# A one-core transformer kernel: each weight split placed by hand in the attention stages, values weighed in two banks in cross, the bias masked a stage earlier

## The chip, the cores and the metric

One NeuronCore of a Trainium2 chip runs the whole program in one launch. The metric is the device time of that launch in microseconds (us). Besides TensorE (PE), VectorE (DVE), ScalarE (ACT) and GpSimd (POOL), the sync engine (SP) issues the loads of the weights.

## The reference

Inputs and outputs are float32: x has 256 rows of 1024. Three transformer layers follow each other. Cut to what matters:

```python
x = x + rms_norm(concat(spatial_gating(za), moba_attention(q, k, v), conformer_conv(zc)) @ w_out, g)   # stage moba
x = x + rms_norm(memory_cross_attention(rms_norm(x, g), rms_norm(mem, g), w_xq, w_xkv, w_xo), g)       # cross: 4 heads of 256
x = x + rms_norm(square(relu(rms_norm(x, g) @ w_ff1)) @ w_ff2, g)                                      # relu
for i in range(2):
    x = x + 0.5 * rms_norm(swiglu(rms_norm(x, g), ...), g)                                             # glu0, glu2
    x = x + rms_norm(differential attention of 8 heads (i = 0) or neighbourhood attention of 16 (i = 1), g)  # diff, near
    x = x + 0.5 * rms_norm(swiglu(...), g)                                                             # glu1, glu3
```

Differential attention takes for each head two softmaxes, p0 - lambda * p1, weighs v with it and normalises the result. Neighbourhood attention adds a bias from a table (`na_rpb`) to the scores, and leaves out all keys outside a window.

## The kernel before

The nine stages (moba, cross, relu, glu0, diff, glu1, glu2, near, glu3) run one after the other. All weights come in 226 "chunks" of 128 x 2048 numbers (1 MB). SP loads chunk c into `raw`, one of 7 places, once chunk c - 7 has been used. Each chunk is then split so that products keep float32's accuracy: ACT copies it to `w_hi` (L612, one of 4 places, so it waits until chunk c - 4 has been used), and DVE writes `w_lo` = `raw` - `w_hi` in place over `raw` (L841). PE multiplies three times, hi by hi, lo by hi, hi by lo (L1169 to L1171). A chunk of the attention stages is used in two halves of 12 matmuls, for rows 0 to 127 and for rows 128 to 255 of x; `qc0.0` in the plan is the first half of a chunk of q's weights, `o1.1` the second half of the out product's chunk 1.

The order of everything is written out by hand in `PLAN`, one string of words for each stage. Every engine walks the same string and does what a word asks of it, waiting on semaphores for the others. Besides the chunks, these words matter here:

- `s`: both engines split the next chunk (ACT hi, DVE lo); `h`: only ACT's half; `l`: only DVE's half. Both count chunks by themselves.
- For an attention unit u (a head): `S` scores (PE), `M` their maximum (DVE, L1031), `E` exp (ACT, L671), `N` probabilities (DVE, L1053), `P` their transposes (PE, L1235), `Q` copy to `probT` (ACT, L679), `W` values weighed (PE, L1250 or L1258 or L1271), `O` the result split to `yT_hi` (ACT) and `yT_lo` (DVE, L1080). In diff also `A` squares (ACT), `B` norm (POOL, then DVE), `Z` transposes of the result (PE).
- `rq`, `rk`, `rv`: rows of q, k or v leave PSUM on ACT; in diff DVE then turns q and k by the rotary angles (L1095 to L1101, "rope"); `tq`, `tk`: their transposes (PE, L1401) and ACT's copy of these.
- `post`, `gain`, `sq`, `turn`: the norms between two stages. `conv_out`: the convolution's Silu (ACT, L716), its hi part (ACT, L719) and lo part (DVE) into the tiles of yT which only the out product's chunk 3 reads.

`attention()` and `attention_pairs()` write the words of the units: step s of diff holds O of unit s - 5, then S of s, W of s - 3, P of s - 2, M, A, Q, E, N, B, the chunks given for that step in `fill`, and Z of s - 4. `used_up` counts the chunks that a step ends, and the next step gets as many splits, all at one place: in diff and cross `s` between B (or N) and the chunks. cross gives all values to one PSUM bank, `OUT_BANK`, so W of unit u waits for `O` of unit u - 1. The bias of near is loaded by POOL in 128 small DMAs during relu, glu0, glu1 and glu2, and masked by POOL in near's head (16 instructions, L592).

Of the kernel before, what the change touches and what calls it, by code (L numbers as in the profile page):

```python
# [40 lines left out]


def attention(kind, units, fill, carry=0):

    words = []
    last = 5 if kind == "diff" else 3
    for s in range(units + last):
        def unit(names, lag):  # L50
            words.extend(f"{name}{s - lag}" for name in names if 0 <= s - lag < units)
        early, _, late = fill.get(s, "").rpartition("|")
        if kind == "diff":
            unit("O", 5)
            if s == units + last - 1:
                break
        unit("S", 0)
        unit("W", 3)
        words += early.split()
        unit("P", 2)  # L60
        unit("M", 0)
        unit("A" if kind == "diff" else "O", 3)
        unit("Q", 2)
        unit("E", 0)
        unit("N", 1)
        if kind == "diff":
            unit("B", 3)
        words += ["s"] * carry
        chunks = late.split()
        words += chunks  # L70
        carry = used_up(early.split() + chunks)
        if kind == "diff":
# [4 lines left out]
def attention_pairs(pairs, fill, carry=0):

    words = []
    for s in range(pairs + 2):
        early, _, late = fill.get(s, "").rpartition("|")
        if s >= 2:
            words += [f"W{s - 2}"]
        if 0 <= s - 1 < pairs:
            words += [f"P{2 * s - 2}"]
        if s < pairs:
            words += [f"S{s}"]
        words += early.split()  # L90
        if 0 <= s - 1 < pairs:
            words += [f"P{2 * s - 1}"]
        if s >= 2:
            words += [f"O{s - 2}"]
        if 0 <= s - 1 < pairs:
            words += [f"Q{2 * s - 2}", f"Q{2 * s - 1}"]
        words += ["h"] * carry
        if s < pairs:
            words += [f"{name}{2 * s + j}" for name in "MEN" for j in range(2)]
        words += ["l"] * carry + late.split()  # L100
        carry = used_up(early.split() + late.split())
    return " ".join(words + ["s"] * carry) + " "

# [11 lines left out]
HEAD_QK = ("qa0.0 post1 s qb0.0 gain1 s sq1 rq0.0 ka0.0 turn1 kb0.0 tq0.0 rk0.0 qa0.1 s qb0.1 tk0.0 rq0.1 s ka0.1 "  # L115
           "tq0.1 s kb0.1 rk0.1 s va0.0 tk0.1 va0.1 s ")
PLAN = {
    "moba": ("g0 s a0 s mem s glu consts u0 s lambda taps0 w0 s gate_norm taps1 K0 s taps2 K1 s gate_scale taps3 K2 s "
             "taps4 K3 s mix taps5 V0 s mix_raw taps6 V1 s taps7 V2 s V3 s conv_mean mix_out conv_sq q0 s conv_var "
             "k0 s conv_root v0 " +  # L120
             attention_pairs(4, {0: "q1", 1: "conv_out k1", 2: "v1", 3: "o0", 4: "o3.0|o3.1", 5: "o1.0"}, 1) +
             "o2.0 post0 gain0 o1.1 turn0 sq0 o2.1"),
    "cross": ("qa0.0 post1 s qb0.0 gain1 s sq1 rq0.0 qc0.0 turn1 qd0.0 tq0.0 rq1.0 qa0.1 s qb0.1 tq1.0 rq0.1 s qc0.1 "
              "tq0.1 s qd0.1 rq1.1 s " +
              attention("cross", 4, {0: "tq1.1|", 4: "o0.0", 5: "o0.1", 6: "o1.0"}) +
              "o2.0 o3.0 post0 gain0 o1.1 s o2.1 turn0 sq0 o3.1"),
    "relu": RELU + "post0 gain0 da6.1 s db6.1 turn0 sq0 s da7.1 db7.1",
    "glu0": GLU + "post0 gain0 da4.1 s db4.1 turn0 sq0 d5.1",
    "diff": (HEAD_QK +
             attention("diff", 8, {0: "vb0 rv0", 1: "qc0 qd0.0", 2: "qd0.1 rq1 kc0.0 tq1 kc0.1",  # L130
# [5 lines left out]
    "near": (HEAD_QK +
             attention_pairs(8, {0: "vb0 rv0", 1: "qc0 qd0.0", 2: "qd0.1 rq1 kc0.0 tq1 kc0.1",
                                 3: "kd0.0 rk1.0 kd0.1 tk1.0 rk1.1 vc0.0 tk1.1", 4: "vc0.1 vd0.0", 5: "vd0.1 rv1 o0.0",
                                 6: "o0.1", 7: "o1.0", 8: "o1.1|o2.0a", 9: "o2.0b"}) +
             "o3.0 post0 gain0 o2.1 turn0 sq0 o3.1"),  # L140
# [1393 lines left out]
```

## Time and profile before

| | |
|---|---|
| median of 3 runs | 1458.69 us (1457.83 to 1461.46) |
| the profiled execution | 1458.49 us, span 1456.7 us |
| PE busy, share of the span | 1394.8 us, 96% |
| DVE, ACT, POOL busy | 839.3, 703.8, 145.9 us |
| mean granted clock of TensorE | 0.991 |

How to read it: a matmul's busy time overlaps the next one's, and its end is modelled, so a busy share of 96% does not say that 4% is all that PE loses. Idle time of PE before an instruction, with the engine that released it, is in the view of the waits; the granted clock is 1 at 2.4 GHz and 0.5 at 1.2 GHz.

### The profile page before, as it was taken

Reading aid. Unit: us, or ns where it says so; the run is one execution under the profiler, and the core shown is the slowest. Engines: PE = TensorE matmul, PEld = TensorE weight load, DVE = VectorE, ACT = ScalarE, POOL = GpSimd, SP = SyncE. Lnnn points to the kernel's source line nnn. Section 1 sums busy time; section 2 is a strip of 40 time slices with the busy share of each in tenths; the row PEclk is TensorE's granted clock in tenths of the full one; section 3 lists DMA queues with packets and bytes.
Section 4 is the critical chain, followed back from the end, with each engine's and each line's share of the span. In section 5 each row is a group of like instructions: output and inputs, shape, how many; then the busy total and the mean of one; then the engine's idle time right before and its main releaser. Section 6 shows DMA issues by size and latency. Waiting matters only on the chain.

```text
span 1456.7 us, 17560 instructions
## 1 busy us (share of the span) xinstructions
PE 1394.8 (96%) x7129; PEld 1166.2 (80%) x7129; DVE 839.3 (58%) x904; ACT 703.8 (48%) x908; POOL 145.9 (10%) x248
## 2 busy tenths in 40 slices
PE   6999989999999999997799999999999999999996
PEld 6998778788888888876678888888888866788885
DVE  4978646645565444654665545655455768655452
ACT  5647454544445434564545343553434566543441
POOL 1000101100001110100111010010100700000000
PEclk9999999999999999999999999999999999999998
DMA  9843334765548556552347656576565534365540
GB/s 314 269 161 136 131 130 143 239 200 187 182 156 252 193 193 195 171 173 88 101 130 225 205 181 206 164 220 205 183 204 168 194 116 131 105 233 197 180 138 30
DMA packets 123421, 255.86 MB, mean 176 GB/s; under 512 B 6280, under 2 KB 36812, under 8 KB 123340
## 3 DMA queue, kind: packets, MB, share of 16 engines
q1 hardware_dynamic: 119244, 251.58, 53.3%
q0 software_dynamic: 4096, 3.15, 0.8%
q8 instruction: 57, 0.93, 0.3%
q14 instruction: 24, 0.20, 0.1%
HBM read 253.66 MB, written 1.05 MB: 175 GB/s over the span
## 4 chain that ended last, share of the span: by engine, by line
PE 88%; DVE 4%; ACT 4%; issue 2%; DMA 1%; POOL 0%; SPq 0%; DVEq 0%; POOLq 0%; ACTq 0%
PE ps L1169 26%; PE ps L1171 26%; PE ps L1170 26%; PE ps L1432 2%; ACT w_hi L612 2%; DVE w_lo L841 1%; ACT t L671 1%; PE ps L1157 1%; PE ps L1159 1%; PE ps L1158 1%; PE ps L1235 1%; PE ps L1198 1%; PE ps L1188 1%; DVE top L1031 1%; DMA raw<-w_in 1%
## 5 line engine op out<-in xcount | busy, mean ns | idle before, releaser
L841 DVE TENSOR_TENSOR w_lo<-raw,w_hi 128x2048 fp32r<-128x2048 f32 x226 | 521.0, 2309 | 435.6 <-ACT w_hi L612 435.1
L612 ACT CAST w_hi<-raw 128x2048 fp32r<-128x2048 f32 x226 | 430.2, 1908 | 393.0 <-PE ps L1171 383.1
L1169 PE MATMUL ps<-w_hi,hT_hi 128*128 128x512 f32 (+1 forms) x1168 | 444.2, 380 | 0.3
L1171 PE MATMUL ps<-w_hi,hT_lo 128*128 128x512 f32 (+1 forms) x1168 | 438.2, 375 | 0.0
L1170 PE MATMUL ps<-w_lo,hT_hi 128*128 128x512 f32 (+1 forms) x1168 | 437.7, 375 | 0.0
L1169 PE MATMUL ps<-w_hi,yT_hi 128*128 128x512 f32 (+1 forms) x672 | 258.8, 385 | 3.5 <-DVE yT_lo L1080 2.0
L1171 PE MATMUL ps<-w_hi,yT_lo 128*128 128x512 f32 (+1 forms) x672 | 255.6, 380 | 0.0
L1170 PE MATMUL ps<-w_lo,yT_hi 128*128 128x512 f32 (+1 forms) x672 | 255.3, 380 | 0.0
L1169 PEld LDWEIGHTS ps<-w_hi,hT_hi 128*128 128x128 f32 x1168 | 220.9, 189 | 41.7 <-DVE w_lo L841 3.7
L1171 PEld LDWEIGHTS ps<-w_hi,hT_lo 128*128 128x128 f32 x1168 | 220.9, 189 | 39.9
L1170 PEld LDWEIGHTS ps<-w_lo,hT_hi 128*128 128x128 f32 x1168 | 221.1, 189 | 37.1
L1169 PEld LDWEIGHTS ps<-w_hi,yT_hi 128*128 128x128 f32 x672 | 126.9, 189 | 27.8 <-DVE w_lo L841 4.3
L1171 PEld LDWEIGHTS ps<-w_hi,yT_lo 128*128 128x128 f32 x672 | 126.7, 189 | 24.4
L1170 PEld LDWEIGHTS ps<-w_lo,yT_hi 128*128 128x128 f32 x672 | 126.9, 189 | 22.8
L534 POOL DMA_DIRECT2D big<-na_rpb x128 | 66.1, 518 | 498.4 <-PE ps L1171 498.4
L546 POOL TENSOR_SCALAR rstd<-ssq 128x1 f32<-128x1 f32 x38 | 17.3, 455 | 659.5 <-ACT probT L618 641.7
L793 ACT ACTIVATE att_bias<-ps,rstd 128x512 f32<-128x512 f32 (+1 forms) x64 | 42.5, 664 | 70.7 <-PE ps L1171 70.6
L1114 DVE SCALAR_TENSOR_TENSOR prob<-ps,rstd,att_bias 128x512 f32<-128x512 f32 (+1 forms) x64 | 45.6, 714 | 26.4 <-PE ps L1171 17.1
L879 DVE SCALAR_TENSOR_TENSOR t<-ps,gain 128x512 f32<-128x512 f32 x36 | 24.7, 690 | 42.5 <-ACT probT L618 42.5
L618 ACT ACTIVATE probT<-ps 128x512 f32<-128x512 f32 x36 | 21.5, 597 | 48.8 <-PE ps L1171 48.8
L636 ACT CAST hT_hi<-ps 128x512 fp32r<-128x512 f32 x36 | 19.8, 589 | 46.6 <-PE ps L1188 46.0
L1122 DVE TENSOR_TENSOR yT_lo<-ps,yT_hi 128x512 fp32r<-128x512 f32 (+1 forms) x64 | 38.9, 648 | 2.9 <-ACT yT_hi L799 2.9
(154 smaller groups left out, 1063.9 us busy)
## 6 DMA issues: line engine op xcount, KB each, us to landing
raw<-ffn_wg SPq DMA_DIRECT2D x44, 1024.0 KB, 5.5
raw<-ffn_wu SPq DMA_DIRECT2D x44, 1024.0 KB, 5.5
raw<-ffn_wd SPq DMA_DIRECT2D x44, 1024.0 KB, 5.3
raw<-w_ff SPq DMA_DIRECT2D x32, 1024.0 KB, 5.9
raw<-diff_w_in SPq DMA_DIRECT2D x12, 1024.0 KB, 5.1
raw<-na_w_in SPq DMA_DIRECT2D x12, 1024.0 KB, 5.2
raw<-w_in SPq DMA_DIRECT2D x10, 1024.0 KB, 5.8
raw<-w_xkv SPq DMA_DIRECT2D x8, 1024.0 KB, 10.9
```

The source lines that it names most:

```text
L534: pool.dma_start(bias[p:p + 1], bass.AP(rpb.tensor, (5 - r) * 31 + 15 - c, [[465, 16], [31, 6], [1, 64]])).then_inc(bias_in, 16)
L612: act.copy(hi_part(c), raw[:, c % NRAW, :]).then_inc(hi_done, 1)
L618: act.activation(dump[:, b, :], src, ACT.Square, scale=1.0 / 32, accum_out=acc).then_inc(done, 1)
L793: act.activation(gate[:, t, 0:width], src[:, 0:width], ACT.Relu if kind == "relu" else ACT.Silu, scale=rstd[:, k:k + 1]).then_inc(gate_don ...
L841: dve.tensor_tensor(lo_part(c), raw[:, c % NRAW, :], hi_part(c), ALU.subtract).then_inc(lo_done, 1)
L879: dve.scalar_tensor_tensor(t1[:, t, half_row], ps[:, 2 * t + b, :], half.get(j, 1.0), gain[:, 0, half_row], ALU.mult, ALU.mult).then_inc(y ...
L1114: dve.scalar_tensor_tensor(hraw[:, t, 0:width], up_bank(kind, b, t)[:, 0:width], rstd[:, k:k + 1], gate[:, t, 0:width], ALU.mult, ALU.mult ...
L1122: dve.tensor_tensor(yT[1][:, part, rows], up_bank(kind, b, t)[:, 0:P * len(tiles)].rearrange("p (k s) -> p k s", k=len(tiles)), yT[0][:, p ...
L1169: pe.matmul(o, hi, wh[:, i, cols], start=first and i == 0, stop=False)
L1170: pe.matmul(o, hi, wl[:, i, cols], start=False, stop=False)
L1171: ins = pe.matmul(o, lo, wh[:, i, cols], start=False, stop=last and i == len(tiles) - 1)
L1432: ins = pe.transpose(up_bank(kind, b, t)[:, cols], hraw[:, t, cols], ident)
```

## The change

The generators lose `used_up`, and each step's fill names up to four places, parted by bars, in which hi and lo splits stand by themselves:

```diff
-def attention(kind, units, fill, carry=0):
+def attention(kind, units, fill):
+    order = {"cross": "S0 .1 P2 W3 M0 Q2 .2 E0 O3 N1 .3 .4", "diff": "O5 S0 W3 P2 .1 M0 A3 Q2 .2 E0 N1 B3 .3 .4 Z4"}[kind]
     words = []
...
-    "diff": (HEAD_QK +
-             attention("diff", 8, {0: "vb0 rv0", 1: "qc0 qd0.0", 2: "qd0.1 rq1 kc0.0 tq1 kc0.1",
...
+             attention("diff", 8, {0: "||l|vb0 rv0", 1: "||h l|qc0 qd0.0 rq1.0", 2: "||h|qd0.1 rq1.1 l kc0.0 tq1 kc0.1",
...
-HEAD_RELU = ("ua0.0 post1 s ub0.0 gain1 s ua1.0 turn1 sq1 ub1.0 G0.0 H0.0 ua0.1 s ub0.1 G0.1 H0.1 s ua1.1 s T0 "
+HEAD_RELU = ("ua0.0 post1 s ub0.0 gain1 s ua1.0 turn1 sq1 ub1.0 G0.0 H0.0 ua0.1 s ub0.1 G0.1 H0.1 s ua1.1 T0 s "
```

What the new words come to, stage by stage:

- diff: the lo split lags one chunk behind the hi split from step 3 on. The first unit's `M0 E0` stand before the lo split instead of after it. `rq1` is parted, its first half one step earlier. Step 3 has no split before `rk1.0`, where there were two; one `h` stands before `tk1.1`. From step 5 on each chunk comes half a chunk or a whole step earlier (`vd0` whole in step 5, `o0.0` in step 6, and so on), and `Z6 O6 Z7 O7` stand together, where `o2.0a` stood between Z6 and Z7.
- near: one split less at step 3, `M` of the first pair before the lo split, no lo split at one later step.
- cross: order `S P W M Q E O N` in place of `S W P M O Q E N`; splits moved behind the units' steps.
- moba: chunk o1 is used before o3, and `conv_out` moves from before `k1` to after `h` at the end of the steps.
- The lo split of the second chunk of the next stage stands after `turn0 sq0` in moba, cross, diff and near.
- relu: `T0` stands before the split, not after it.

In cross unit u odd gets its own bank, bank 4, which is free of scores once E of unit 2 is done:

```diff
+        def out_bank(kind, u):
+            return ps[:, 4 if kind == "cross" and u % 2 else OUT_BANK, :]
...
-                        if u:
-                            pe.wait_ge(o_lo, a["e0"] + u)
+                        if u == 1:
+                            pe.wait_ge(e_ready, u0 + 3)
+                        if u >= 2:
+                            pe.wait_ge(o_lo, a["e0"] + u - 1)
```

The last 32 bias loads are spread over 18 chunks of glu2 instead of 27, and the mask follows there, at the end of its chunk 20 of 33:

```diff
-                            if 27 * p // 32 == i:
+                            if (18 if kind == "glu2" else 27) * p // 32 == i:
...
-                    if kind == "near" and word.name == "rk" and (word.digit, word.half) == (0, 0):
+                    if kind == "glu2" and word.c == FIRST[word.at] + 20 and word.done:
+                        pool.wait_ge(used, word.c + 1)
                         pool.wait_ge(bias_in, 16 * P)
```

Three places show how instructions move. The first is ACT in moba: the casts to `w_hi` are hi splits, `big<-big,par` is conv_out's Silu, `kT<-ps` is the evacuation of k1, `probT<-ps` is Q. Before:

```order
L671 ACTIVATE t,denom<-att_bias,neg_top 128x256 x4
L716 ACT_TABLE_LOAD
L716 ACTIVATE big<-big,par 128x256 x2
L719 CAST yT_hi<-big 128x512
L750 COPY kT<-ps 128x512
L699 CAST yT_hi<-ps 128x256
L679 COPY probT<-ps 128x512 x2
L612 CAST w_hi<-raw 128x2048
L671 ACT_TABLE_LOAD
L671 ACTIVATE t,denom<-att_bias,neg_top 128x256 x4
```

Of the change, in the last steps of moba:

```order
L671 CAST yT_hi<-ps 128x256
L651 COPY probT<-ps 128x512 x2
L584 CAST w_hi<-raw 128x2048
L688 ACT_TABLE_LOAD
L688 ACTIVATE big<-big,par 128x256 x2
L691 CAST yT_hi<-big 128x512
L671 CAST yT_hi<-ps 128x256
L584 CAST w_hi<-raw 128x2048
L590 ACTIVATE probT,ssq<-ps 128x512 x2
```

and where cross' first exp stands now, the end of its query rows:

```order
L749 ACTIVATE gain<-ps,rstd 128x512
L736 COPY qT<-ps 128x4x128
L643 ACT_TABLE_LOAD
L643 ACTIVATE t,denom<-ps,neg_top 128x256 x4
L651 COPY probT<-ps 128x512
```

Silu and its load of a table have gone from ahead of `kT<-ps` to behind a hi split at the stage's end, and the load that brought Exp back stands before the first exp of cross.

The second is PE in cross: `ps<-big,qT` are scores (8 records: two units), `ps<-tab,prob` is P, `ps<-probT,big` is W. Before, from S1 and S2 on:

```order
L1208 MATMUL ps<-big,qT 128x256 x8
L1235 MATMUL ps<-tab,prob 128x128 x4
L1208 MATMUL ps<-big,qT 128x256 x4
L1258 MATMUL ps<-probT,big 128x256 x4
L1235 MATMUL ps<-tab,prob 128x128 x4
L1258 MATMUL ps<-probT,big 128x256 x4
L1235 MATMUL ps<-tab,prob 128x128 x4
```

Of the change:

```order
L1180 MATMUL ps<-big,qT 128x256 x8
L1207 MATMUL ps<-tab,prob 128x128 x4
L1180 MATMUL ps<-big,qT 128x256 x4
L1207 MATMUL ps<-tab,prob 128x128 x4
L1232 MATMUL ps<-probT,big 128x256 x4
L1207 MATMUL ps<-tab,prob 128x128 x4
L1232 MATMUL ps<-probT,big 128x256 x4
```

P1 now stands before W0, and P2 before W1.

The third is DVE in diff, from N2 in step 3 to M4 in step 4: `prob<-t` is N, `att_bias<-ps,sub_stat` is B, `gain` and `att_bias<-gain` are the rope of k. Before:

```order
L1053 SCALAR_TENSOR_TENSOR prob<-t,inv_denom 128x256 x2
L1065 SCALAR_TENSOR_TENSOR att_bias<-ps,sub_stat,sub_gain 128x128 x2
L841 TENSOR_TENSOR w_lo<-raw,w_hi 128x2048 x2
L1095 TENSOR_TENSOR att_bias<-gain,tab 128x8x8
L1097 TENSOR_TENSOR att_bias<-gain,tab 128x8x8
L1100 TENSOR_TENSOR gain<-gain,tab 128x8x16
L1101 TENSOR_TENSOR gain<-gain,att_bias 128x8x16
L1095 TENSOR_TENSOR att_bias<-gain,tab 128x8x8
L1097 TENSOR_TENSOR att_bias<-gain,tab 128x8x8
L1100 TENSOR_TENSOR gain<-gain,tab 128x8x16
L1101 TENSOR_TENSOR gain<-gain,att_bias 128x8x16
L1031 TENSOR_REDUCE top<-ps 128x4
```

Of the change:

```order
L1025 SCALAR_TENSOR_TENSOR prob<-t,inv_denom 128x256 x2
L1037 SCALAR_TENSOR_TENSOR att_bias<-ps,sub_stat,sub_gain 128x128 x2
L1067 TENSOR_TENSOR att_bias<-gain,tab 128x8x8
L1069 TENSOR_TENSOR att_bias<-gain,tab 128x8x8
L1072 TENSOR_TENSOR gain<-gain,tab 128x8x16
L1073 TENSOR_TENSOR gain<-gain,att_bias 128x8x16
L1067 TENSOR_TENSOR att_bias<-gain,tab 128x8x8
L1069 TENSOR_TENSOR att_bias<-gain,tab 128x8x8
L1072 TENSOR_TENSOR gain<-gain,tab 128x8x16
L1073 TENSOR_TENSOR gain<-gain,att_bias 128x8x16
L1003 TENSOR_REDUCE top<-ps 128x4
```

Both lo splits that stood ahead of the rope of k are gone from here.

## Rows read from the trace of the kernel before

**Rows 1.** The page, part 1: busy us of the engines (share of the span), instructions.

```profile
PE 1394.8 (96%) x7129; PEld 1166.2 (80%) x7129; DVE 839.3 (58%) x904; ACT 703.8 (48%) x908; POOL 145.9 (10%) x248
```

**Rows 2.** Waits of PE: who, released by whom: us in total, times, longest.

```profile
PE ps L1235 <- DVE yT_lo L1080: 7.5, 3, 3.4
PE ps L1401 <- DVE gain L1101: 7.5, 4, 4.5
PE ps L1235 <- DVE prob L1056: 4.3, 3, 2.4
...
PE ps L1208 <- ACT t L671: 2.9, 1, 2.9
...
PE ps L1198 <- ACT kT L750: 1.5, 1, 1.5
PE ps L1169 <- DVE yT_lo L1122: 1.4, 1, 1.4
...
PE ps L1198 <- ACT t L671: 1.0, 1, 1.0
```

**Rows 3.** Sums by window: PE, PEld, DVE, ACT, POOL busy, granted clock, DMA share, GB/s.

```profile
671.40:691.40 20.00, 14.78 (x66) 11.62 (x65) 9.62 (x19) 8.99 (x19) 1.03 (x2) 0.83 0.16 53
691.40:742.90 51.50, 41.85 (x225) 33.62 (x225) 30.34 (x60) 28.54 (x81) 8.76 (x14) 0.93 0.36 113
941.20:1128.50 187.30, 187.27 (x902) 157.31 (x901) 100.53 (x74) 82.63 (x77) 19.93 (x41) 1.00 0.61 195
1159.00:1254.80 95.80, 88.55 (x469) 65.68 (x469) 68.15 (x138) 56.51 (x116) 3.92 (x5) 0.98 0.37 118
```

**Rows 4.** Timeline of ACT, then one row of PE, moba: start us, us, instruction, idle before.

```profile
126.82 1.28 ACT L716 ACT_TABLE_LOAD   x1
128.12 1.09 ACT L716 ACTIVATE big<-big,par 128x256 f32<-128x256 f32 x2
...
129.76 0.58 ACT L750 COPY kT<-ps 128x512 f32<-128x512 f32 x1
...
151.44 0.59 ACT L679 COPY probT<-ps 128x512 f32<-128x512 f32 x1 [2.60 <-PE ps L1235]
...
155.12 0.50 PE L1169 MATMUL ps<-w_hi,yT_hi 128*128 128x512 f32 x1
```

**Rows 5.** Timeline of PE, diff: same columns; a matmul at half clock among them.

```profile
685.41 0.63 PE L1170 MATMUL ps<-w_lo,hT_hi 128*128 128x512 f32 x1
...
691.40 1.13 PE L1198 MATMUL ps<-kT,qT 64*128 64x256 f32 x8 [0.72 <-issue]
...
701.33 0.63 PE L1235 MATMUL ps<-tab,prob 128*128 128x128 f32 x4 [2.11 <-DVE yT_lo L1080]
...
742.86 0.47 PE L1169 MATMUL ps<-w_hi,yT_hi 128*128 128x512 f32 x1 [2.02 <-DVE yT_lo L1080]
```

**Rows 6.** By line, 691 to 743 us (diff): xcount | busy us, mean ns | idle.

```profile
L841 DVE TENSOR_TENSOR w_lo<-raw,w_hi 128x2048 fp32r<-128x2048 f32 x5 | 11.5, 2292 | 8.6 <-ACT w_hi L612 8.6
L612 ACT CAST w_hi<-raw 128x2048 fp32r<-128x2048 f32 x5 | 9.6, 1915 | 0.0
...
L671 ACT ACTIVATE t<-ps,neg_top 128x256 f32<-128x256 f32 x16 | 7.4, 481 | 0.0
...
L1031 DVE TENSOR_REDUCE top<-ps 128x4 f32<-128x1024 f32 x4 | 4.9, 1216 | 5.1 <-PE ps L1198 5.1
...
L1080 DVE TENSOR_TENSOR yT_lo<-ps,yT_hi 128x256 fp32r<-128x256 f32 x8 | 3.4, 420 | 7.6 <-ACT yT_hi L692 7.6
```

**Rows 7.** Timeline of POOL, then of DVE, start of near: the mask and the splits.

```profile
1138.25 23.80 POOL L592 TENSOR_TENSOR big<-big,tab 128x384 f32<-128x384 f32 x16
...
1150.15 9.10 DVE L841 TENSOR_TENSOR w_lo<-raw,w_hi 128x2048 fp32r<-128x2048 f32 x3 [0.95 <-ACT w_hi L612]
```

**Rows 8.** Timeline of PE, cross: scores of unit 2, values of unit 1.

```profile
200.37 1.97 PE L1208 MATMUL ps<-big,qT 128*128 128x256 f32 x8 [2.95 <-ACT t L671]
...
207.72 1.97 PE L1258 MATMUL ps<-probT,big 128*128 128x256 f32 x8 [1.06 <-DVE yT_lo L1080]
```

More of the change, by code:

```diff
@@ L25 @@
 FAR = 1e30
-def used_up(chunks):
-    return sum(word[0] in "qkvo" and word[-2:] not in (".0", "0a", "0b", "1a") for word in chunks)
-def attention(kind, units, fill, carry=0):
+def attention(kind, units, fill):
+    order = {"cross": "S0 .1 P2 W3 M0 Q2 .2 E0 O3 N1 .3 .4", "diff": "O5 S0 W3 P2 .1 M0 A3 Q2 .2 E0 N1 B3 .3 .4 Z4"}[kind]
     words = []
[L48 to L74, printed above, removed]
@@ L77, in attention_pairs @@
-def attention_pairs(pairs, fill, carry=0):
+    for s in range(units + {"cross": 3, "diff": 5}[kind]):
+        parts = [part.strip() for part in fill.get(s, "|||").split("|")]
+        for token in order.split():
+            if token[0] == ".":
+                words.append(parts[int(token[1:]) - 1])
+            elif 0 <= s - int(token[1:]) < units:
+                words.append(f"{token[0]}{s - int(token[1:])}")
+    return " ".join(words) + " "
+def attention_pairs(pairs, fill):
     words = []
@@ L82, in attention_pairs @@
     for s in range(pairs + 2):
[L83 to L102, printed above, removed]
+        parts = [part.strip() for part in fill.get(s, "|||").split("|")]
+        now, last, out = s < pairs, 0 <= s - 1 < pairs, s >= 2
+        words += [f"W{s - 2}"] * out + [f"P{2 * s - 2}"] * last + [f"S{s}"] * now + [parts[0]] + [f"P{2 * s - 1}"] * last
@@ L105 @@
+        words += [f"O{s - 2}"] * out + [f"Q{2 * s - 2} Q{2 * s - 1}"] * last + [parts[1]]
+        words += [f"{name}{2 * s} {name}{2 * s + 1}" for name in "MEN"] * now + parts[2:]
+    return " ".join(words) + " "
 HEAD_GLU = ("ga0.0 post1 s gb0.0 gain1 s ua0.0 turn1 sq1 ub0.0 G0.0 H0.0 ga0.1 s gb0.1 G0.1 s ua0.1 s "
@@ L115 @@
 HEAD_QK = ("qa0.0 post1 s qb0.0 gain1 s sq1 rq0.0 ka0.0 turn1 kb0.0 tq0.0 rk0.0 qa0.1 s qb0.1 tk0.0 rq0.1 s ka0.1 "
-           "tq0.1 s kb0.1 rk0.1 s va0.0 tk0.1 va0.1 s ")
+           "tq0.1 s kb0.1 rk0.1 s va0.0 tk0.1 va0.1 h ")
 PLAN = {
@@ L120 @@
              "k0 s conv_root v0 " +
-             attention_pairs(4, {0: "q1", 1: "conv_out k1", 2: "v1", 3: "o0", 4: "o3.0|o3.1", 5: "o1.0"}, 1) +
-             "o2.0 post0 gain0 o1.1 turn0 sq0 o2.1"),
+             attention_pairs(4, {0: "|h|l|q1", 1: "|h|l|k1", 2: "|h|l|v1", 3: "|h|l|o0", 4: "o1.0|h conv_out||o1.1",
+                                 5: "|h|l|o3.0"}) +
+             "o2.0 post0 gain0 o3.1 turn0 sq0 l o2.1"),
     "cross": ("qa0.0 post1 s qb0.0 gain1 s sq1 rq0.0 qc0.0 turn1 qd0.0 tq0.0 rq1.0 qa0.1 s qb0.1 tq1.0 rq0.1 s qc0.1 "
-              "tq0.1 s qd0.1 rq1.1 s " +
-              attention("cross", 4, {0: "tq1.1|", 4: "o0.0", 5: "o0.1", 6: "o1.0"}) +
-              "o2.0 o3.0 post0 gain0 o1.1 s o2.1 turn0 sq0 o3.1"),
+              "tq0.1 h qd0.1 rq1.1 " +
+              attention("cross", 4, {0: "tq1.1|||", 4: "|h|l|o0.0", 5: "||l|o0.1", 6: "|h|l|o1.0"}) +
+              "o2.0 o3.0 post0 gain0 o1.1 h o2.1 turn0 sq0 l o3.1"),
     "relu": RELU + "post0 gain0 da6.1 s db6.1 turn0 sq0 s da7.1 db7.1",
@@ L129 @@
     "diff": (HEAD_QK +
-             attention("diff", 8, {0: "vb0 rv0", 1: "qc0 qd0.0", 2: "qd0.1 rq1 kc0.0 tq1 kc0.1",
[3 rows of a table removed]
+             attention("diff", 8, {0: "||l|vb0 rv0", 1: "||h l|qc0 qd0.0 rq1.0", 2: "||h|qd0.1 rq1.1 l kc0.0 tq1 kc0.1",
+                                   3: "|||kd0.0 rk1.0 kd0.1 tk1.0 rk1.1 vc0.0 h tk1.1", 4: "||h l|vc0.1",
+                                   5: "||h l|vd0 rv1", 6: "||h l|o0.0", 7: "||h|o0.1", 8: "||h l|o1.0", 9: "||l|o1.1a",
+                                   10: "||l|o1.1b o2.0a"}) +
+             "h o2.0b o3.0 post0 gain0 o2.1 turn0 sq0 l o3.1"),
     "glu1": GLU + "post0 gain0 da4.1 s db4.1 turn0 sq0 d5.1",
@@ L136 @@
     "near": (HEAD_QK +
[L137 to L140, printed above, removed]
+             attention_pairs(8, {0: "||l|vb0 rv0", 1: "|h|l|qc0 qd0.0 rq1.0", 2: "|h|l|qd0.1 rq1.1 kc0.0 tq1 kc0.1",
+                                 3: "|h|l|kd0.0 rk1.0 kd0.1 tk1.0 rk1.1 vc0.0 h tk1.1", 4: "|h|l|vc0.1 vd0.0",
+                                 5: "|h|l|vd0.1 rv1 o0.0", 6: "|h||o0.1", 7: "|h|l|o1.0", 8: "o1.1||l|o2.0a",
+                                 9: "|h|l|o2.0b"}) +
+             "o3.0 post0 gain0 o2.1 turn0 sq0 l o3.1"),
     "glu3": GLU + "post0 da4.1 db4.1 d5.1 end1",
@@ L695, in unit_word @@
                         act.copy(yT[0][:, 2 * u:2 * u + 2, :],
-                                 ps[:, OUT_BANK, :].rearrange("p (a s) -> p a s", a=2)).then_inc(o_hi, 1)
+                                 out_bank(kind, u).rearrange("p (a s) -> p a s", a=2)).then_inc(o_hi, 1)
                     else:
@@ L1075, in out_lo @@
                     elif kind == "cross":
-                        tiles, src = slice(2 * e, 2 * e + 2), ps[:, OUT_BANK, :].rearrange("p (a s) -> p a s", a=2)
+                        tiles, src = slice(2 * e, 2 * e + 2), out_bank(kind, e).rearrange("p (a s) -> p a s", a=2)
                     else:
@@ L1242, in weigh_values @@
                     pe.wait_ge(pt_ready, u0 + u + 1)
-                    bank = ps[:, OUT_BANK, :]
+                    bank = out_bank(kind, u)
                     if kind == "diff":
```

3 rows, old and new, of the table PLAN are left out of this document.

## The prediction

> **What bounds the kernel now.** I read the page first: PE is busy for 1394.8 of 1456.7 us, DVE for 839.3, ACT for 703.8 [rows 1]. So PE sets the time, and the change gives it no less work; it can only take away time in which PE waits or runs at the lower clock. Second, the waits of PE [rows 2]. The reader is to see that they belong to attention stages: 7.5 us for `yT_lo`, 7.5 for the rope (`gain`), 4.3 for `prob`, 2.9 and 1.0 for exp, 1.5 for k1's copy, and one wait of 1.4 in relu. That is 26.1 us. Third, the windows [rows 3]: granted clock 0.83 over 20.0 us and 0.93 over 51.5 us of diff, 0.98 over 95.8 us of near. At half clock that is (1 - 0.83) x 20.0 / 0.5 = 6.8 us, 7.2 us and 3.8 us, coarse for the last; each fall comes behind a wait of 2 us or more. A matmul then takes 0.63 us, against 0.47 for the one at 742.86 [rows 5]; its clock is 1.2 instead of 2.4 GHz. Nothing else that the change touches lasts long on PE. Half a chunk is 12 matmuls, and takes 2.84 us from its first start to the next word's.
>
> Why PE waits in diff is in one stretch. From S4 at 691.40 to P3 at 701.33 are 9.93 us, 2.11 of them waiting [rows 5]; 7.8 is PE's own work. P3 waits for O0's `yT_lo`, and DVE did a lo split first, 2.29 us, which waited for its hi split, 1.92, which stood behind exp, 4 x 0.48 less overlap = 1.85 us [rows 6].
>
> **The change, part by part.**
>
> *diff, the rope and the first exp.* The waits for `gain` sum to 7.5. In step 3 two hi and two lo splits (3.7 and 4.5 us) stood before `rk1.0` and its rope. Now none does: ACT takes rk1.0 right behind E3, 1.85 us after M3, while PE has two half chunks, 5.7 us, to do; I take that wait, 4.5, as gone. Before tq1 the first half's rope is now done a step earlier, the second still stands behind one hi split: E2 ends 1.85 + 1.2 + 0.2 us after S2's maximum can start, which the first half's rope puts off by 0.7, and hi split, copy and rope add 1.8 + 0.7 + 1.0. Against P0, `qd0.1`, `kc0.0` and half of tq1, that is 1.2 us late. So 6.3 of 7.5 go. M0 and E0 stand before the lo split: the wait of 1.0 goes. Of the wait for tk1.1's copy to ACT nothing goes. Together 7.3.
>
> *diff, the steps from S4 on.* The lo split no longer waits for the hi split of its own place, since it is one chunk behind, and starts right after B. What remains ahead of O0 is ACT's line: scores 1.1, then A, Q (until 3.5), exp 1.85, hi split 1.9, O's hi 0.4 and lo 0.42 [rows 6], 8.2 with the signals, against PE's 7.8. So 0.4 us of waiting in place of 2.11. The same walk over the next steps gives for P4 none (the step has a whole chunk), P5 0.3, P6 1.3 (the hi split stands right ahead of O3), P7 0.4, and 0.4 before `o2.0a`. A new wait comes at the end: Z7 follows Z6 at once, but needs O6's `yT_lo`, which stands behind a lo split: 1.8. `o3.0`, which waited 2.02 [rows 5], finds everything there. In all 4.6 remain where 7.5 + 2.0 stood: 4.9 less.
>
> *diff, the clock.* Its falls cost: `vc0.0` 5.2 against 2.8 us, with its transposes another 0.6, the two falls of 3.4 us in the later stretch 1.75 each, 6.5 us in all. No remaining wait in diff is above 1.8, so I take them as gone. diff: 7.3 + 4.9 + 6.5 = **18.7 us less**.
>
> *near.* M0 and M1 before the lo split take the 2.4 of the 4.3 us for `prob`; one lo split left out of step 7's predecessor takes 0.8 more and leaves 1.1. One split less before `rk1.0` takes 1.4. The fall of the clock behind the 2.4 goes, 1.6 us of work. Less by 2.4 + 0.8 + 1.4 + 1.6 = **6.2**.
>
> *moba.* k1's copy stood behind table load, Silu and cast, 2.94 us from 126.82 to 129.76 [rows 4], and S2 waited for it: 1.5 by the row, 1.75 from start to start. That goes. But `o3.0` now needs conv_out: from Q7's start ACT does 0.5 (Q) + 1.9 (hi split) + 2.94, then DVE its lo part, 0.7 (estimate: 0.42 for half the width), 6.0 us. PE comes to that place 155.12 - 151.44 = 3.7 us after Q7's start [rows 4]. So it waits 2.4 to 2.5. moba: **0.8 more**.
>
> *cross.* S2 at 200.37 waited 2.9 for E0 [rows 8], since a lo split stood before M0. Now M0 is done 0.8 us after S0, but the table load, 1.28 [rows 4], has moved here, and exp of 0.95 follows: S2 at 198.4, 2.0 earlier. The two banks take away W1's wait of 1.06 [rows 8], but P2, now ahead of W1, needs N2, which stands behind O0 on DVE: hi 0.6, lo 0.7, N 0.8 and signals behind W0, a new wait of 2.3. Before, W1 filled 1.8 of that time. Walked to `o1.0`: **0.9 less**. This new wait is where I would expect a look at the order to pay.
>
> *relu.* T0 before the split: its `yT_lo` comes before `da0` needs it. **1.6 less** (1.4 by the row).
>
> *The bias.* POOL's mask took 23.8 us for 16, 1.02 alone and up to 3.07 beside a split; three splits beside it took 9.10, 3.03 each instead of 2.28 [rows 7]. near's head had no wait of PE from that, so nothing is gained there. In glu2 DVE is busy 100.5 of 187.3 us [rows 3]. At worst the mask lasts 16 x 3.07 = 49 us, with 26 us of DVE's own work in it and 16 x 0.75 = 12 more: 38 of 49. It costs nothing; if that cover were gone, up to 12 us. The Trainium skill (SBUF — State Buffer, Who interferes with whom) has it that DVE with two inputs in SBUF and a GpSimd instruction that reads SBUF block each other fully. The row agrees: a split is longer by most of one mask.
>
> *What does nothing.* diff's steps began with the new scores before too: S, W, P stand in the same order on PE. The lo split after `turn0 sq0` delays the next stage's post and gain on DVE by 0.5 to 1.1 us, and `turn1` has 0.6 of room. The loads keep their places, 7 chunks ahead.
>
> **The sum.** -18.7 - 6.2 + 0.8 - 0.9 - 1.6 = -26.6. From the profiled execution, 1458.5, that is 1431.9; it stands 0.2 under the median, so I forecast 1432.0. Bounds: if all the waits I leave (4.6, 2.5, 2.3) vanish, 1422.6. If the steps of diff keep 2.1 us each in place of 0.4, five times, and the clock still falls as often, +8.5 and +8: 1448.
>
> **The rivals.**
>
> *The loop of a unit stays as long as it was.* `O` lo, M, E, hi split, O again, go round through DVE and ACT; if ACT's line is 1.7 us longer than my walk, each of five steps waits 2.1 and the falls of two of them remain: 1432 + 8.5 + 3.5 = 1444. For it: E and the hi split are back to back already. Against: in the step that had no split before, P5 came without any wait. Chance 0.14.
>
> *The clock falls all the same*, behind the new waits of 2.3 to 2.5 in moba and cross and behind small ones: four times 1.7: 1439. Against: S2's wait of 2.9 in cross was followed by no fall. Chance 0.10.
>
> *The load of a table costs more than its row.* The Trainium skill (ScalarE: Activation LUTs, What ACT_TABLE_LOAD costs) gives some 1283 ns and a drain of 1380 for a switch. By that page both new places wait 1.4 longer, and the sum would be 1434.8. The rows speak against a drain: Silu starts 0.02 us behind its load's end [rows 4]. As a mechanism here, from rows: if 1.3 us more came behind each load, of the load's own length, 1432 + 2 x 1.3 = 1434.6. Chance 0.05.
>
> *Slower: the mask holds DVE.* If each of 16 masks blocks DVE for its whole 3.07 us, 49 + 26 us of work stand in 49 us, DVE is 26 us late, and PE waits in glu2, which has no wait now; with three falls of the clock, 5 us, 1463. It starts to cost once a mask delays DVE by more than (49 - 26) / 16 = 1.4 us; the rows say 0.75. Chance 0.03.
>
> **How the numbers follow.** My forecast has 0.65, the rivals 0.32, and 0.03 is for several small ones that together give the gain back. The range takes in the first three and both bounds but for their ends: 1425 to 1446. Nothing under 0.3%, some 4.4 us, can be told from no change. Faster by more: 0.65 + 0.14 + 0.10 + 0.05 = 0.94; within it 0.03; slower 0.03.
>
> **What would show it.** In the new profile: the wait for `gain` at 1.2 or less; no wait for `prob` above 1; in the waits a new one of 2.4 for the conv part of `yT_lo` and one of 2.3 for `prob` in cross; one of 1.8 before Z7; granted clock 1.00 over diff; the mask in glu2 with PE at 100% beside it. I am wrong if PE waits in glu2, if diff takes more than 129 us from its first matmul to glu1's (now 144.6), or if moba's end loses 5 us.

## The result, and the profile after the change

The changed kernel takes **1437.95 us** in the median of 4 runs (1437.1 to 1441.11), against 1459.87 of the kernel before beside it: ratio **0.9855, interval 0.9833 to 0.9876**. It is faster, by 21.9 us; 26.6 were forecast. The profiled execution took 1437.34 us, its span 1435.6 against 1456.7, 21.1 less. The forecast of 1432.0 is 6 us too low; its range of 1425 to 1446 holds the time.

The page of the changed kernel, part 1, beside [rows 1]:

```profile
span 1435.6 us, 17561 instructions
...
PE 1388.4 (97%) x7129; PEld 1162.6 (81%) x7129; DVE 836.2 (58%) x904; ACT 704.5 (49%) x908; POOL 148.2 (10%) x248
```

PE's instructions are the same number, and its busy time fell by 6.4 us. That fits matmuls at half clock that now run at the full one: the lower clock was granted for 26.0 us in all before, and for 11.2 now. The waits of PE, beside [rows 2]:

```profile
PE ps L1141 <- DVE w_lo L813: 3.8, 4, 1.1
PE ps L1207 <- DVE prob L1028: 3.2, 3, 2.1
PE ps L1141 <- DVE yT_lo L937: 2.6, 1, 2.6
...
PE ps L1259 <- DVE yT_lo L1052: 1.9, 1, 1.9
PE ps L1207 <- DVE yT_lo L1052: 1.8, 3, 1.3
PE ps L1180 <- ACT t L643: 1.4, 1, 1.4
PE ps L1375 <- DVE gain L1073: 1.3, 2, 1.0
```

The waits for the rope (7.5 us, now 1.3) and for `yT_lo` in the units' loop (7.5, now 1.8 and 1.9) went as forecast. The third line is moba's new wait for conv_out, the second has cross' new wait of 2.1 for N2. The first line was not forecast: four waits of 1.1 for a lo split.

The windows, columns as in [rows 3]: the first two hold the same work of diff as the two with clock 0.83 and 0.93 before, from S3 to S4 and from S4 to `o3.0`, 12.5 and 43.3 us where 20.0 and 51.5 stood. Then cross, then glu2 with the mask.

```profile
670.70:683.20 12.50, 11.83 (x65) 9.59 (x64) 5.23 (x17) 7.29 (x18) 1.03 (x2) 1.00 0.25 85
683.20:726.50 43.30, 39.11 (x225) 31.45 (x226) 32.35 (x61) 29.55 (x82) 6.48 (x14) 1.00 0.43 134
...
200.00:240.00 40.00, 37.12 (x170) 31.07 (x171) 21.00 (x34) 17.91 (x40) 1.69 (x3) 0.96 0.44 156
858.00:1045.00 187.00, 186.96 (x900) 156.99 (x899) 100.56 (x73) 82.26 (x78) 24.55 (x48) 1.00 0.64 196
```

Most of what follows is read in one number per stage: from the start of PE's first matmul of a stage to that of the next. Stages that a change does not touch agree to 0.1 us from kernel to kernel but for falls of the clock, and but for moba, which varies by up to 1.9 us more between kernels that leave it as it is. So this tells more than the medians, whose executions spread over 0.4 to 5 us.

| stage | before | changed | difference | forecast |
|---|---|---|---|---|
| moba | 150.07 | 151.09 | +1.02 | +0.8 |
| cross | 67.77 | 69.75 | **+1.98** | -0.9 |
| relu | 185.29 | 184.57 | -0.72 | -1.6 |
| glu0 | 187.32 | 187.35 | 0.0 | 0 |
| diff | 144.60 | 125.64 | -18.96 | -18.7 |
| glu1 | 187.33 | 188.23 | **+0.90** | 0 |
| glu2 | 187.31 | 187.36 | 0.0 | 0 |
| near | 129.15 | 122.69 | -6.46 | -6.2 |
| glu3 | 199.11 | 200.01 | **+0.90** | 0 |

The large terms held; 5.5 us were given back in cross, relu, glu1 and glu3. The timeline of DVE, POOL and PE at the start of glu1 shows how (start, duration, instruction, idle before):

```profile
735.98 2.28 DVE L813 TENSOR_TENSOR w_lo<-raw,w_hi 128x2048 fp32r<-128x2048 f32 x1
...
736.67 1.76 POOL L517 TENSOR_SCALAR rstd<-ssq 128x1 f32<-128x1 f32 x1 [5.57 <-ACT probT L590]
...
740.16 1.42 DVE L860 SCALAR_TENSOR_TENSOR x_rows<-t,rstd,x_rows 128x512 f32<-128x512 f32 x2 [0.70 <-POOL rstd L518]
...
741.50 2.28 DVE L813 TENSOR_TENSOR w_lo<-raw,w_hi 128x2048 fp32r<-128x2048 f32 x1
...
743.83 0.50 PE L1141 MATMUL ps<-w_hi,hT_hi 128*128 128x512 f32 x1 [0.93 <-DVE w_lo L813]
```

The lo split that the change put behind `turn0 sq0` runs from 735.98 on. POOL's root of one column takes 1.76 us beside it. The norm (`x_rows`) comes at 740.16, the next split stands behind it, and the third chunk's first matmul waits for that split, 0.93 by the row. The norm's own row says which of the two delays set it: DVE was free again 0.70 us before, and waited for POOL.

### The profile page after: what moved, and what is told of

Its sections match the earlier page's. It is cut to its first block, busy times and chain, and to the rows that moved or that the text cites. A ratio compares the mean times of both kernels' runs of the same rounds, so it can differ in the third digit from the quotient of the medians.

```text
span 1435.6 us, 17561 instructions
## 1 busy us (share of the span) xinstructions
PE 1388.4 (97%) x7129; PEld 1162.6 (81%) x7129; DVE 836.2 (58%) x904; ACT 704.5 (49%) x908; POOL 148.2 (10%) x248
## 3 DMA queue, kind: packets, MB, share of 16 engines
HBM read 253.66 MB, written 1.05 MB: 177 GB/s over the span
## 4 chain that ended last, share of the span: by engine, by line
PE 90%; ACT 3%; DVE 3%; issue 2%; POOL 1%; DMA 1%; SPq 0%; DVEq 0%; POOLq 0%; ACTq 0%
PE ps L1141 26%; PE ps L1143 26%; PE ps L1142 26%; PE ps L1406 2%; PE ps L1129 2%; PE ps L1130 1%; PE ps L1131 1%; PE ps L1170 1%; PE ps L1207 1%; DVE w_lo L813 1%; PE ps L1160 1%; ACT t L643 1%; ACT w_hi L584 1%; POOL rstd L517 1%; DMA raw<-w_in 1%
## 5 line engine op out<-in xcount | busy, mean ns | idle before, releaser
L1141 PEld LDWEIGHTS ps<-w_hi,yT_hi 128*128 128x128 f32 x672 | 126.5, 188 | 26.6 <-issue 3.6
L517 POOL TENSOR_SCALAR rstd<-ssq 128x1 f32<-128x1 f32 x38 | 21.2, 559 | 687.4 <-ACT probT L590 669.1
```

What stands on the lines that cost most here:

```text
L517: link(pool.tensor_scalar(rstd[:, k:k + 1], ssq[:, k, 0:1], ssq[:, k, 1:2], EPS, ALU.add, ALU.add))
L1141: pe.matmul(o, hi, wh[:, i, cols], start=first and i == 0, stop=False)
```

## The experiments

All change the changed kernel, but for what is said. Each is compared by stage with it, from one profiled execution; the ratios are those to the kernel before, which ran beside.

### The lo split behind `turn0 sq0`

In moba, cross and diff it moves ahead of `post0`; in near it stays:

```diff
-                                  5: "|h|l|o3.0"}) +
-             "o2.0 post0 gain0 o3.1 turn0 sq0 l o2.1"),
+                                  5: "|h|l l|o3.0"}) +
+             "o2.0 post0 gain0 o3.1 turn0 sq0 o2.1"),
...
-              "o2.0 o3.0 post0 gain0 o1.1 h o2.1 turn0 sq0 l o3.1"),
+              "o2.0 o3.0 post0 gain0 o1.1 s o2.1 turn0 sq0 o3.1"),
...
-              "h o2.0b o3.0 post0 gain0 o2.1 turn0 sq0 l o3.1"),
+              "s o2.0b o3.0 post0 gain0 o2.1 turn0 sq0 o3.1"),
```

> The changed kernel, with the lo split of the next stage's second chunk taken from behind turn0 sq0 and put earlier in moba, cross and diff (near keeps it). My theory: that split costs 1.1 us at the start of each of four stages, because it holds up DVE's post1 (and POOL's root beside it, 1.76 us in place of 0.30), and with it the lo split of the third chunk. So the first stretch of cross, relu and glu1 (first two half chunks) gets back from 6.5 to 5.65 us, glu3's stays: 3.3 us less than the changed kernel in all. Rival: the wait at the stage heads comes from PE running ahead of the loads of the weights; then moving the split changes nothing, and PE still waits 1.1 us for w_lo in all four.

Measured: 1436.73 us (1436.17 to 1437.62), ratio 0.9844 (0.983 to 0.9859). relu takes 183.51 (1.06 less), glu1 187.33 (0.90 less, what it took before the change), and cross 67.31, 2.44 less, of which 1.6 is a fall of the clock that is missing here (below). glu3, where near's split was left, stays at 199.99; in the run with near's old words (below), in which that split stands elsewhere, it takes 199.09. In the waits one of the four for `w_lo` is left:

```profile
PE ps L1141 <- DVE w_lo L813: 0.9, 1, 0.9
```

And at the start of glu1, the root and the norm (same columns as above):

```profile
736.53 0.30 POOL L517 TENSOR_SCALAR rstd<-ssq 128x1 f32<-128x1 f32 x1 [5.56 <-ACT probT L590]
...
739.13 1.41 DVE L860 SCALAR_TENSOR_TENSOR x_rows<-t,rstd,x_rows 128x512 f32<-128x512 f32 x2 [0.35 <-POOL rstd L518]
```

The root takes 0.30 us where no split runs beside it. So the place of this one split costs 0.8 to 1.1 us in each stage behind it. It acts in two ways: DVE's queue is 2.28 us longer, and POOL's reply comes later, since the first root ends 1.46 us later and the second stands behind it. The reply weighs more. Of the 0.9 us by which the norm is late in glu1, DVE had its queue done 0.70 us before the reply came. The time as a whole gained only 1.2 us; in the profiled execution the clock fell in moba and diff, where it had not in the changed kernel's.

### conv_out one step earlier

```diff
-3: "|h|l|o0", 4: "o1.0|h conv_out||o1.1",
+3: "|h|l|conv_out o0", 4: "o1.0|h||o1.1",
```

> The changed kernel, with conv_out one step earlier, before chunk o0, where ACT and DVE have time. My theory: the wait of PE for conv's lo part, 2.6 us, is ACT's line of a hi split, a table load and Silu behind Q7; moved earlier it goes, and moba takes 148.6 us in place of 151.1. The move back of k1's copy stays. Rival: ACT is full in that step too, and PE waits there for O2 or P6 instead: moba stays within 1 us of 151.1.

Measured: 1434.77 us (1433.48 to 1437.65), ratio 0.9833 (0.9818 to 0.9848). The wait of 2.6 for `yT_lo L937` is gone from PE's waits. moba takes 149.61, 1.48 less than in the changed kernel. Word by word only W3 with what waits behind it is shorter, 1.01 us instead of 3.65, and nothing behind it is longer; K0, K1 and V3, well ahead of the edit, were 1.0 us longer in this execution, a variation that kernels without this edit have too. So the edit gives back the whole 2.64, and where the clock falls behind that wait, 1.6 more.

### cross: N ahead of O, and the second bank

```diff
-    order = {"cross": "S0 .1 P2 W3 M0 Q2 .2 E0 O3 N1 .3 .4",
+    order = {"cross": "S0 .1 P2 W3 M0 Q2 .2 E0 N1 O3 .3 .4",
```

> The changed kernel, with N before O in a step of cross. My theory: P2's wait of 2.1 to 2.5 us is N2 behind O0 on DVE; with N first it goes, and with it the fall of the clock that comes right behind it (3.4 us at 1.2 GHz, some 1.7 us of work): cross takes 65.6 in place of 69.8 us. Rival one: the fall has another cause and stays: 67.3. Rival two: W1 then waits for what stood behind N, and cross keeps within 1 us of 69.8.

Measured: 1435.68 us (1434.76 to 1436.5), ratio 0.9837 (0.9822 to 0.9851). cross takes 65.70 us, 4.05 less than in the changed kernel. PE in the changed kernel, from P1 on (start, duration, instruction, idle before):

```profile
204.72 0.60 PE L1207 MATMUL ps<-tab,prob 128*128 128x128 f32 x4
205.16 1.89 PE L1232 MATMUL ps<-probT,big 128*128 128x256 f32 x8
209.18 1.10 PE L1207 MATMUL ps<-tab,prob 128*128 128x128 f32 x4 [2.12 <-DVE prob L1028]
210.07 3.17 PE L1232 MATMUL ps<-probT,big 128*128 128x256 f32 x8
```

and with N first:

```profile
206.28 0.60 PE L1207 MATMUL ps<-tab,prob 128*128 128x128 f32 x4
206.72 1.89 PE L1232 MATMUL ps<-probT,big 128*128 128x256 f32 x8
208.45 0.60 PE L1207 MATMUL ps<-tab,prob 128*128 128x128 f32 x4
208.89 1.89 PE L1232 MATMUL ps<-probT,big 128*128 128x256 f32 x8
```

The wait of 2.12 is gone, 2.5 us from start to start, and so is what stood behind it: the same eight matmuls of W1 took 3.17 us at the lower clock (1.2 GHz) and take 1.89 at 2.4.

What the two banks are worth was asked in both orders:

```diff
-            return ps[:, 4 if kind == "cross" and u % 2 else OUT_BANK, :]
+            return ps[:, OUT_BANK, :]
...
-                        if u == 1:
-                            pe.wait_ge(e_ready, u0 + 3)
-                        if u >= 2:
-                            pe.wait_ge(o_lo, a["e0"] + u - 1)
+                        if u:
+                            pe.wait_ge(o_lo, a["e0"] + u)
```

> cross weighs its values in one bank again, with the changed order. Theory: the second bank is worth nothing in this order, because N2, for which P2 waits, stands behind O0 on DVE, so O0 is done before W1 comes anyway: cross stays at 69.7 us (within 0.3, without a difference in falls of the clock). Rival: W1 waits about 1.1 us again and cross takes 70.8.

> cross with N ahead of O on DVE, in one bank; beside it stands the run with N ahead of O and two banks, where cross took 65.70 us and P2 did not wait. Theory: now W1 comes before O0 is out of the bank and waits 1.0 to 1.4 us, so cross takes 66.8 to 67.2: the second bank pays only in this order. Rival: 65.7, the bank is worth nothing in either order.

Measured, one execution each: 1440.93 and 1438.61 us. With O first cross takes 69.77 (two banks: 69.75). With N first it takes 67.01 (two banks: 65.70), and PE waits ahead of W1:

```profile
211.02 1.32 PE L1230 MATMUL ps<-probT,big 128*128 128x256 f32 x5 [1.05 <-DVE yT_lo L1052]
```

So the second bank is worth nothing in the order of the change, since P2's wait for N2 lets O0 finish anyway, and 1.3 us once N stands first.

### diff: two splits back ahead of the rope

```diff
-3: "|||kd0.0 rk1.0 kd0.1 tk1.0 rk1.1 vc0.0 h tk1.1", 4: "||h l|vc0.1",
-5: "||h l|vd0 rv1",
+3: "||h l h l|kd0.0 rk1.0 kd0.1 tk1.0 rk1.1 vc0.0 tk1.1", 4: "|||vc0.1",
+5: "||h|vd0 rv1",
```

> Only diff changes: in its third step two hi splits and two lo splits stand ahead of kd0.0 and rk1.0 again, as before the change; all other stages and all other steps of diff stay as changed. Theory (the term of 4.5 us, with part of the 6.5 for the clock, is the splits ahead of the rope): PE waits 3.5 to 4.7 us for the rope ahead of tk1.0 and the clock falls behind it; diff goes from 125.6 to 131 to 133.5 us, every other stage within 0.3 us but for falls of the clock. Rival (the gain came from the scores' order and the first exp, the place of the splits is worth little): the wait is under 1.5 us and diff stays under 128.

Measured: 1446.58 us (1444.89 to 1448.69), ratio 0.9909 (0.989 to 0.9928). diff takes 133.07, 7.43 more. PE ahead of tk1.0 (same columns):

```profile
685.69 0.82 PE L1375 MATMUL ps<-tab,gain 128*128 128x128 f32 x4 [4.49 <-DVE gain L1073]
686.16 0.78 PE L1141 MATMUL ps<-w_hi,hT_hi 128*128 128x512 f32 x1
686.73 0.63 PE L1142 MATMUL ps<-w_lo,hT_hi 128*128 128x512 f32 x1
```

The wait of 4.5 of [rows 2] is back, with half clock behind it. It makes 4.65 from start to start, the clock 1.6 in tk1.0 and `vc0.0`; another 1.6 is a fall at the stage's end, behind the wait for Z7, that all but one of the other kernels with this wait show too; P3's wait of 0.4 goes. So this one place holds 5.8 us, a little under a third of diff's gain. The rest was not tested by itself.

### near's old words; the mask back in near

The first gives near the words of the kernel before, with the mask in glu2; the second keeps the new words and puts the mask back:

```diff
+PLAN["near"] = ('qa0.0 post1 s qb0.0 gain1 s sq1 rq0.0 ka0.0 turn1 kb0.0 tq0.0 rk0.0 qa0.1 s qb0.1 tk0.0 rq0.1 '
...
```

```diff
-                    if kind == "glu2" and word.c == FIRST[word.at] + 20 and word.done:
-                        pool.wait_ge(used, word.c + 1)
+                    if kind == "near" and word.name == "rk" and (word.digit, word.half) == (0, 0):
```

> near has the words of the kernel before, all else as changed; the bias mask stays in glu2. Theory: near takes 129.1 us, 6.5 more than the changed kernel's 122.7, since its words alone made the gain, and glu3 takes 1.0 less (199.1), since its third chunk's lo split no longer stands behind turn0. Rival (the mask in near's head made part of near's time before): near stays under 128.5 us.

> The bias mask is back in near's head, on POOL behind rk0.0; all else as changed. The run with near's old words and the mask in glu2 took 127.27 us for near, 1.88 less than the kernel before with the same words. Theory: with the changed order M0 and M1 stand ahead of the lo split, so the mask delays nothing that PE waits for: near stays at 122.7 (within 0.3) and glu2 at 187.3. Rival: the mask still stretches the DVE work ahead of P0, and near takes 0.8 to 1.9 us more, 123.5 to 124.6.

Measured: 1443.72 us (1440.7 to 1445.42), ratio 0.9893 (0.9872 to 0.9913), and 1439.89 (1438.94 to 1441.2), ratio 0.9876 (0.9855 to 0.9897). With its old words near takes 127.27 us, not 129.15: the rival holds for 1.88 us. The kernel before, last split and first P of near:

```profile
1161.03 3.17 DVE L841 TENSOR_TENSOR w_lo<-raw,w_hi 128x2048 fp32r<-128x2048 f32 x1 [1.79 <-ACT w_hi L612]
...
1168.15 1.11 PE L1235 MATMUL ps<-tab,prob 128*128 128x128 f32 x4 [2.42 <-DVE prob L1056]
```

and the same with the mask in glu2:

```profile
1145.13 2.29 DVE L824 TENSOR_TENSOR w_lo<-raw,w_hi 128x2048 fp32r<-128x2048 f32 x1 [3.10 <-ACT w_hi L595]
...
1151.38 0.66 PE L1218 MATMUL ps<-tab,prob 128*128 128x128 f32 x4 [1.54 <-DVE prob L1039]
```

The split is 0.88 us shorter without the mask beside it, the wait 0.88 shorter, and no fall of the clock follows (P 0.66 instead of 1.11); that fall makes the other 1.0. With one execution of each it is not shown that the mask brought the fall. With the new words the mask costs nothing in near (122.68), because M0 and M1 no longer stand behind that split. So in the old order the mask cost 0.9 us, and perhaps the fall; in the new order either of the two places is free, and two parts of the change had bought the same microsecond.

### diff's end: o2.0a or o2.0b ahead of Z7

```diff
-                                   10: "||l|o1.1b o2.0a"}) +
+                                   10: "||l|o1.1b", 11: "|||o2.0a"}) +
```

```diff
-                                   10: "||l|o1.1b o2.0a"}) +
-             "h o2.0b o3.0 post0 gain0 o2.1 turn0 sq0 l o3.1"),
+                                   10: "||l|o1.1b o2.0a", 11: "|||o2.0b"}) +
+             "h o3.0 post0 gain0 o2.1 turn0 sq0 l o3.1"),
```

> The changed kernel, with chunk o2's first quarter between Z6 and Z7 in diff, as before the change, and O6 ahead of it. My theory: the wait of 1.9 us before Z7 goes, since 1.4 us of matmuls cover it, and 0.3 to 0.5 remain: diff takes 124.1 in place of 125.6 us. Rival: the lo split ahead of O6 sets the time; then PE waits as long behind the quarter, at o3.0 or Z7: 125.6.

> In diff o2.0b moves ahead of Z7, so that PE has 1.48 us of work between the start of the last unit's chain and Z7; all else as changed. The run that moved o2.0a behind Z6 gave nothing, since the work ahead of Z7 stayed the same in sum. Theory: the wait of 1.9 us before Z7 shrinks to 0.4 to 0.6, no fall of the clock follows it, and diff takes 124.0 to 124.4 us. Rival: the wait moves on to o3.0, whose last rows come as late, and diff stays at 125.4 to 127.3.

Measured: 1440.73 us (1439.54 to 1441.08), ratio 0.9869 (0.9852 to 0.9885), and 1438.87 (1437.17 to 1440.18), ratio 0.987 (0.9852 to 0.9889). The first is a miss: the wait is as long. What counts is PE's work between the scores and values of the last unit and Z7, and that did not change. Of the second, PE at Z7 and at `o3.0`:

```profile
727.72 0.41 PE L1259 MATMUL ps<-tab,att_bias 128*128 128x128 f32 x2 [0.54 <-DVE yT_lo L1052]
729.14 0.47 PE L1141 MATMUL ps<-w_hi,yT_hi 128*128 128x512 f32 x1 [1.01 <-DVE yT_lo L1052]
```

The wait of 1.92 became 0.54 and 1.01: `o3.0` needs the last unit's `yT_lo` as well, and `o2.0b`, which hid that, was used up. diff takes 125.53 us: as much as the changed kernel's without a fall, 1.7 less than its 127.2 with one. The rival holds for the wait. Only the fall is missing, here and in the kernel of the next part, which has the same words.

### All that gained, together

> All moves that gained, in one kernel: the lo split of the next stage's second chunk ahead of post0 in moba, cross, diff and now near; conv_out one step earlier; N ahead of O in cross; o2.0b ahead of Z7. By the stage lengths seen: moba 149.6, cross 64.6, relu 183.5, diff 124.1, glu1 187.3, near 122.7, glu3 199.0, 11 us less than the changed kernel's profiled span of 1435.6: span 1424.5, time 1426.2 us, without a fall of the clock before the end. Rival (gains shift to the next wait): above 1431.

Measured: **1428.72 us** (1428.59 to 1429.0), ratio **0.9802 (0.9785 to 0.9819)**, profiled span 1426.8. It beats both kernels. Its edit is the diffs above (the lo splits with near's too, conv_out, N first, o2.0b). By stage: moba 149.99, cross 64.81, relu 183.51, diff 125.45, glu1 187.33, near 122.99, glu3 199.09. The span is 2.3 us over what was expected: 1.35 in diff by the wait that moved on to `o3.0`, 0.3 in near, where a wait for the norm between the stages (DVE `t`) is 0.9 instead of 0.6 behind two lo splits in a row, 0.4 in moba, where the clock fell for 3.4 us at 19 us into the program (1.5 us of work). What is left of PE's waits beyond the first line, which is the start of the program:

```profile
PE ps L1158 <- DVE att_bias L835: 10.5, 1, 10.5
PE ps L1160 <- DVE t L826: 4.3, 6, 0.9
...
PE ps L1207 <- DVE yT_lo L1052: 1.7, 3, 1.3
PE ps L1180 <- ACT t L643: 1.4, 1, 1.4
```

### When the clock falls

In the changed kernel a fall to the lower clock lasts 3.4 us and costs about 1.6. (In the kernel before, the one behind the wait of 4.5 for the rope lasted 6.8.) But for the first 25 us and the last 11 of the program, the new order has it at three places only, each behind a wait of about 2 us, and not every time. The counts are over the profiled executions of the changed kernel and of the experiments that keep the wait:

| wait of PE | us | followed by a fall | stage without and with it, all else equal |
|---|---|---|---|
| for conv_out, moba | 2.6 | 6 of 10 | 151.1 and 152.7 |
| P2's, cross | 2.1 | 7 of 9 | 68.2 and 69.75 |
| Z7's, diff | 1.9 | 9 of 10 | 125.6 and 127.2 |

The changed kernel's profiled execution has it in cross alone, the run with the split moved in moba and diff but not in cross, the one with near's old words in diff alone. The changed kernel's four executions have a mean clock of 0.996, 0.996, 0.993 and 0.994 at 1437.34, 1437.1, 1441.11 and 1438.56 us. The kernel with everything together has none of the three waits, a clock of 0.996 in all four, and they lie within 0.41 us.

That the spread is the falls is argued from these, not tested by itself, and it is not all of it. In kernels that edit nothing in moba, its words up to the last W take 134.4 to 136.4 us, the longest in an execution in which the clock did not fall in moba at all, and the program reaches its first chunk at 18.7 to 19.6 us. The cause of that part is open.

## Why the prediction was right, and where it was not

- **diff, -18.7; measured -18.96.** Right, by its own steps. Up to S4 10.6 us went (7.3 of waits and 3.0 for the clock in `vc0.0` were forecast), behind it 8.4 (4.9 and 3.5). The waits that it left are there, from start to start: 1.22 before tq1 (forecast 1.2), 0.39 before P3 (0.4), 0.38 before P5 (0.3), 1.40 before P6 (1.3), 0.2 before P7 (0.4) and 2.09 before Z7 (1.8); one of 0.45 before W7 it did not name. The term of 4.5 for the rope is shown by the run that put the splits back; the other terms are read from the two traces, not tested by themselves. "I take them as gone" of the clock's falls was true of the profiled execution, and that was luck in part: the wait before Z7 was followed by one in each of the nine experiments' profiles that keep it. With it diff takes 127.2, 17.4 less than before.
- **near, -6.2; measured -6.46.** The sum was right, its reasons were not quite. The text said of the mask that "near's head had no wait of PE from that, so nothing is gained there." The run with the old words shows that 0.9 us of the 2.4 us wait came from the mask; the fall behind it is missing there too. The new order alone would have taken both, so the sum did not suffer.
- **moba, +0.8; measured +1.02.** Right: the wait of 2.4 to 2.5 for conv_out is 2.6.
- **cross, -0.9; measured +1.98.** The new wait of 2.3 before P2 is 2.1 by the row and 2.5 from start to start. What was missed is 1.6 for the clock behind it, 0.8 for the lo split behind moba's `turn0`, and 0.4 at S2, which comes 1.6 us earlier and not 2.0 (its wait is 1.4 in the table of waits). The rival in which the clock falls all the same was right about this place. Its price of four falls was too high: kernels that keep all three waits show one to three. That the profiled execution had a single one is luck in part.
- **The step that failed** is "The lo split after `turn0 sq0` delays the next stage's post and gain on DVE by 0.5 to 1.1 us, and `turn1` has 0.6 of room." turn1 was the wrong one to ask. The next lo split stands behind post and gain on DVE, and the third chunk needs it. Also POOL's root, which the norm waits for, takes 1.76 instead of 0.30 us beside the split, and by the norm's row this is the larger part. That step was costed at 0 and measured 0.8 to 1.1 in each of four stages, 3.7 in sum. The price could have been read: in the trace of the kernel before a root beside two-input instructions of DVE takes 1.05 us in cross (at 174.69) and 3.34 in near (at 1134.31), with no wait of PE behind it. In relu it made -0.7 of what was forecast as -1.6; without it relu gains 1.8, which is the term for T0.
- **A reading.** The 0.63 us of a matmul at half clock was set beside 0.47 [rows 5]. That 0.47 is the first matmul behind a wait. The like of it at half clock is 0.78, the row ahead of the 0.63 in the run with the splits back; the like of the 0.63 at full clock is 0.39 (at 734.78 in the changed kernel). No term was worked out from it.
- **The bias mask, 0; measured 0.** glu2 takes 187.36 (187.31), PE is at 100%. The mask's row and one split beside it:

```profile
1044.04 23.91 POOL L564 TENSOR_TENSOR big<-big,tab 128x384 f32<-128x384 f32 x16 [15.60 <-PE ps L1143]
...
1045.98 3.18 DVE L813 TENSOR_TENSOR w_lo<-raw,w_hi 128x2048 fp32r<-128x2048 f32 x1 [3.14 <-ACT w_hi L584]
```

The mask lasts as long as in [rows 7], and the cover, DVE's idle time in glu2, is there. The slower rival, a mask that blocks DVE for its whole length, fell. So did the loop that stays as long (P3 waits 0.4, not 2.1) and the drain behind a load of a table: cross' first exp starts at 199.59 us, 0.02 behind its load's end, and moba's Silu 0.01 behind its own.

The miss of 5.5 us in the span is 3.7 for the split in four stages, 1.6 for one fall of the clock, 0.4 at S2 in cross and 0.2 in moba, less 0.5 that diff and near gave beyond the forecast.

## What to carry to other kernels

Where an operation is moved on an engine with a queue, ask for every later consumer on that queue, not only for the one that is next, and for what another engine does beside it that the queue will wait for: here the first consumer had room and the third did not, and most of its delay came by way of POOL's reply. When a wait is filled by moving work, count what work lies between the producer's start and the wait; moving a piece within that stretch gives nothing, and taking it from behind lets the next wait appear. A wait of 2 us is worth more than its length, here 1.6 us more when the clock falls behind it. The kernel with none of these waits in moba, cross and diff is also the one whose executions lie closest together.
